# The first solve's base products ahead of the SSD stage's last products, its first inverses before the key weights

## The reference, cut to what matters

```python
xn = _rms_norm(h, pre_mix_norm[l])
proj = (xn @ w_in[l]).astype(jnp.float32)
y_ssd = _ssd_mixer(p_ssd, ...)       # chunks of 128; y * silu(z), then a norm by groups
y_rwkv = _rwkv7_mixer(p_rwkv, ...)   # the recurrence below
mix = jnp.concatenate([y_ssd, y_rwkv], axis=-1) @ w_out[l]
...
def step(S, inp):                    # _rwkv7_scan, 256 steps, 8 heads of 64
    sa = jnp.einsum("bhij,bhj->bhi", S, a_t)
    S = S * w_t[:, :, None, :] + sa[..., None] * b_t[:, :, None, :] + v_t[..., None] * k_t[:, :, None, :]
    return S, jnp.einsum("bhij,bhj->bhi", S, r_t)
```

## Time and profile before

| what | before |
|---|---|
| median of 3 runs | 737.87 us (737.47 to 738.0) |
| the profiled execution | 737.89 us |
| its span, first to last instruction | 736.1 us |
| TensorE busy | 725.6 us, 99% |
| VectorE busy | 563.6 us, 77% |
| ScalarE busy | 435.3 us, 59% |
| GpSimd busy | 49.4 us, 7% |
| granted TensorE clock, mean | 0.998 |

### The profile page before, as it was taken

The page is one execution under the profiler, slowest core; times in us unless marked ns, Lnnn a source line. Parts: engine busy times, 40 slices in busy tenths (PEclk is TensorE's granted clock), DMA queues, the critical chain, the costliest instruction groups (busy, mean ns, idle before and its releaser), DMA issues.

```text
span 736.1 us, 16703 instructions
## 1 busy us (share of the span) xinstructions
PE 725.6 (99%) x7176; PEld 592.3 (80%) x7176; DVE 563.6 (77%) x895; ACT 435.3 (59%) x689; POOL 49.4 (7%) x83
## 2 busy tenths in 40 slices
PE   9999999999999999999999999999999999999997
PEld 7888877888788888888878695898888888865553
DVE  5789978777789999997568787889685676762453
ACT  5699863425748666766557572487473755653342
POOL 0000133040020000000002000003003000000000
PEclk9999999999999999999999999999999999999999
DMA  9990205320666655565771732338335354566001
GB/s 316 394 410 10 113 19 219 129 88 31 231 232 224 218 181 180 225 225 177 280 292 36 288 138 112 116 126 333 116 124 219 106 211 170 203 229 234 24 1 58
DMA packets 67146, 129.51 MB, mean 176 GB/s; under 512 B 3968, under 2 KB 28032, under 8 KB 66816
## 3 DMA queue, kind: packets, MB, share of 16 engines
q1 hardware_dynamic: 66032, 126.07, 46.9%
q0 software_dynamic: 320, 1.67, 0.6%
q10 hardware_dynamic: 720, 0.70, 0.3%
HBM read 127.39 MB, written 1.05 MB: 174 GB/s over the span
## 4 chain that ended last, share of the span: by engine, by line
PE 91%; DVE 6%; issue 1%; ACT 1%; ACTq 0%; DVEq 0%
PE bank L626 44%; PE bank L748 14%; PE bank L3205 11%; PE bank L2531 3%; PE bank L1570 3%; PE bank L1551 2%; PE bank L883 1%; DVE arena L572 1%; PE bank L1829 1%; PE bank L902 1%; PE bank L2008 1%; DVE arena L614 1%; PE bank L828 1%; PE bank L2745 1%; PE bank L3028 1%
## 5 line engine op out<-in xcount | busy, mean ns | idle before, releaser
L626 PE MATMUL bank<-hg,arena 128*128 128x256 f16 x2496 | 275.0, 273 | 0.2 <-DVE hg L651 0.2
L626 PEld LDWEIGHTS bank<-hg,arena 128*128 128x128 f16 x2496 | 243.9, 98 | 30.5 <-issue 1.1
L572 DVE SCALAR_TENSOR_TENSOR arena<-ring,arena 128x1024 f16<-128x1024 f32 x150 | 175.6, 1226 | 59.1 <-ACT arena L540 59.1
L540 ACT ACTIVATE arena<-ring 128x1024 f16<-128x1024 f32 x150 | 146.7, 1044 | 86.8 <-PE bank L3205 37.6
L3205 PE MATMUL bank<-arena 128*128 128x512 f16 (+1 forms) x480 | 83.6, 336 | 0.0
L3205 PEld LDWEIGHTS bank<-arena 128*128 128x128 f16 x480 | 47.0, 98 | 36.1
L748 PE MATMUL bank<-arena 128*128 128x256 f16 x528 | 57.8, 273 | 0.0
L748 PEld LDWEIGHTS bank<-arena 128*128 128x128 f16 x528 | 51.7, 98 | 6.0
L559 DVE SCALAR_TENSOR_TENSOR arena<-ring,arena 128x2048 f16<-128x2048 f32 x22 | 50.4, 2292 | 0.7
L748 PE MATMUL bank<-mix,arena 128*128 128x256 f16 x384 | 42.2, 273 | 0.0
L552 ACT ACTIVATE arena<-ring 128x2048 f16<-128x2048 f32 x22 | 41.7, 1894 | 0.0
(11 more groups left out here) (420 smaller groups left out, 971.1 us busy)
## 6 DMA issues: line engine op xcount, KB each, us to landing
ring<-in_w_in_dram SPq DMA_DIRECT2D x12, 2048.0 KB, 8.9
ring<-in_ffn_w_up_dram SPq DMA_DIRECT2D x22, 1024.0 KB, 7.2
ring<-in_w_ff_dram SPq DMA_DIRECT2D x8, 2048.0 KB, 9.2
ring<-in_w_ff_dram SPq DMA_DIRECT2D x16, 1024.0 KB, 6.4
ring<-in_ffn_w_down_dram SPq DMA_DIRECT2D x11, 1024.0 KB, 5.2
ring<-in_w_out_dram SPq DMA_DIRECT2D x8, 1024.0 KB, 7.9
ring<-in_w_xk_dram SPq DMA_DIRECT2D x2, 2048.0 KB, 11.6
ring<-in_w_xv_dram SPq DMA_DIRECT2D x2, 2048.0 KB, 10.1
```

The lines of the kernel that those rows point to most:

```text
L540: nc.scalar.activation(quarter(halves_of(chunk)[0], chunk, q), quarter(slot(*chunk), chunk, q), ACT.Copy, scale=W_SCALE).then_inc(*mark("w ...
L572: nc.vector.scalar_tensor_tensor(quarter(halves_of(chunk)[1], chunk, q), quarter(slot(*chunk), chunk, q), W_SCALE, quarter(halves_of(chunk ...
L626: mm = nc.tensor.matmul(out_, weight[a][:, k, cols], src[:, k, b, :], start=(first and i == 0), stop=(last and i == 2), skip_group_check=True)
```

## The change

On TensorE, the base products of chunk 0 move from behind `products` to a place between z tile 3 and the SSD products of chunk 1, with three waits before them. On VectorE, all four memory tiles 4 to 7 come before z's eviction, the first inverses of both groups come before the low half of key quarter 0, and the negated blocks become a step of their own, "lower blocks", behind that low half. Level 0's product waits for that step too. In chunk 1 the order of VectorE's work stays as it was.

```diff
             for c in range(NC_):
                 if c:
                     pe_z_tile(pe, 3)
+                    pe.wait_ge(*at("k token-major"))
+                    pe.wait_ge(*at("ssd state out"))
+                    pe.wait_ge(*at("AT"))
+                    base_products(0)
                 for g in range(2):
                     pe.wait_ge(*at("ssd mt", c, g))
...
-            dve_mem_low16(dve, (4,))
+            dve_mem_low16(dve, (4, 5, 6, 7))
             dve_z(dve, 1)
-            dve_mem_low16(dve, (5, 6, 7))
+            for g in range(2):
+                dve_first_inverse(dve, 0, g)
             mem_low(dve, 0)
+            for g in range(2):
+                dve_lower_blocks(dve, 0, g)
...
             products(c, 0, BT, AT_, "LT bank")
-            if c == 0:
-                base_products(c)
             fill(0)
...
                     if n == 0:
                         pe.wait_ge(*at("LT", c, g))
+                        pe.wait_ge(*at("lower blocks", c, g))
...
+        def base_blocks(g):
+            return banks[3 * g + 1][:, 0:4 * BASE].rearrange("p (j n) -> p j n", j=4)
+
+        def dve_lower_blocks(dve, c, g):
+            if c:
...
+                return
+            dve.wait_ge(*at("ssd y", 1, 1))
+            nc.vector.tensor_scalar(LT32[g], base_blocks(g), -1.0, None, ALU.mult).then_inc(
+                *mark("solve_vector", "lower blocks", c, g))
+
+        def dve_first_inverse(dve, c, g, between=lambda: None):
+            st = sets[g]
+            dve.wait_ge(*at("blocks bank", c, g))
+            if c:
+                dve.wait_ge(*at("XT diagonal", 0, g))
+            nc.vector.tensor_tensor(st["XT"], base_blocks(g), over(const("pair32"), 4), ALU.mult).then_inc(
+                *mark("solve_vector", "XT pairs", c, g))
+            between()
+            dve.wait_ge(*at("XT pairs", c, g))
+            nc.vector.tensor_tensor(st["XT"], st["XT"], over(const("ident32"), 4), ALU.add).then_inc(
+                *mark("solve_vector"))
+            dve.wait_ge(*so_far("solve_vector"))
+            nc.vector.transpose(flat(st["X"]), flat(st["XT"])).then_inc(*mark("solve_vector", "X", c, g, 0))
+
         def dve_rwkv_chunk(dve, c):
-            for g in range(2):
...
+            if c:
+                for g in range(2):
+                    dve_first_inverse(dve, c, g, lambda: dve_lower_blocks(dve, c, g))
             for n, m in enumerate(LEVELS):
```

More of the change, by code:

```diff
@@ L2018, in even @@
             return v.rearrange("p (b two m) -> p b two m", two=2, m=m)[:, :, 0, :]
-        def dve_rwkv_chunk(dve, c):
-            for g in range(2):
[L2022 to L2042, removed]
@@ new lines, in base_blocks @@
+        def base_blocks(g):
+            return banks[3 * g + 1][:, 0:4 * BASE].rearrange("p (j n) -> p j n", j=4)
+        def dve_lower_blocks(dve, c, g):
+            if c:
+                nc.vector.tensor_tensor(
+                    LT64[g].rearrange("p j (two n) -> p j two n", two=2),
+                    base_blocks(g).unsqueeze(2).broadcast_to([P, 4, 2, BASE]),
+                    const("blocks64").rearrange("p (two n) -> p two n", two=2).unsqueeze(1).broadcast_to(
+                        [P, 4, 2, BASE]), ALU.mult).then_inc(*mark("solve_vector", "lower blocks", c, g))
+                return
+            dve.wait_ge(*at("ssd y", 1, 1))
+            nc.vector.tensor_scalar(LT32[g], base_blocks(g), -1.0, None, ALU.mult).then_inc(
+                *mark("solve_vector", "lower blocks", c, g))
```

## The result

The changed kernel takes 739.49 us (median of 13 runs, 739.03 to 741.27), the kernel before 737.87 (13 runs, 737.35 to 738.44): a ratio of 1.0026, 95% interval 1.0018 to 1.0033. By the medians it is slower by 1.62 us, and 739.6 was forecast. (The medians' quotient is 1.0022.

What follows compares the result with a forecast made beforehand. TensorE, busy 99% of the span, was taken as the bound, with VectorE on the chain from 101.15 to 107.25 us. Terms +0.61, +1.72, -0.18 and -0.39 gave +1.76 on 737.89: 739.65, about 739.6 as median; range 738.4 to 740.3.

Steps and rivals of the forecast that it cites:

- The step on which all hangs: VectorE's tile 5, issued behind GpSimd's r by k product, stands until 96.08 and takes about 2.5 us instead of 0.48.
- Rival A: VectorE's memory tiles do not stand behind GpSimd, so the kernel is not slower: -0.27 us, 737.6; chance 0.08.
- Rival B: VectorE keeps the port, GpSimd waits, and the first "plus identity" stands until 97.24: +0.88 us, 738.8; chance 0.12.
- Rival C: A later wait swallows part of the loss, or a term is too large: +0.5 to +1.4 us, 738.4 to 739.3; chance 0.12.
- Rival D: The 1.75 us wait costs TensorE its clock, half quarter 2.84 instead of 1.42: +1.4 us more, 741; chance 0.04.
- z +0.61: On VectorE, z's eviction comes behind the memory tiles instead of hidden under GpSimd's product: +0.61 us.
- inverses +1.72: On VectorE, both first inverses run ahead of the low half that TensorE's next product waits for: +1.72 us.
- the nearer hand-over -0.18: From the low half's end to TensorE's use of it takes 0.06 us instead of 0.24: -0.18 us.
- level 0 -0.39: TensorE's level 0 of both groups runs back to back, 0.73 us instead of 1.12: -0.39 us.
- packed: From 101.15 us on VectorE is busy for 5.91 of 6.05 us, so everything behind moves together by the shift.

Runs made afterwards that it cites:

- the tiles only: The kernel before, with only the three memory tiles 5 to 7 moved ahead of z's eviction: 739.10 us against 737.64, ratio 1.0026.
- the inverses only: The changed kernel with memory tiles 5 to 7 back behind z, so only base products and first inverses are early: 738.88 us against 737.64 for the kernel before.
- the low half first: The changed kernel with key quarter 0's low half put ahead of the first inverses on VectorE: 739.07 us against 737.75 for the kernel before, ratio 1.0017.
- the product twice: The changed kernel with GpSimd's product r*k' issued twice in a row: 743.55 us against 737.75 for the kernel before, ratio 1.0087.

## Why the prediction was right

All steps are counted from tile 4's start (0.48 later in the profile after). z's eviction was forecast 3.70 us behind it and came 3.69 behind. The two inverses were put at 1.72 and took 1.72. The low half was to end at 7.24 and ended at 7.19. TensorE's wait for z was put at 0.35 and was 0.40; that for the low half at 1.75 and was 1.58. The level-0 run of 64 began at 8.67, where 8.72 was forecast. The shift of the second key quarter was put at 1.76 and was 1.70, and 1.62 of it showed in the median.

The step on which all hangs, that tile 5 stands until GpSimd's product is through, held as written, with 2.58 us for a tile against the 2.5 named. That the product is the cause was shown from both sides: held back, the four tiles take 1.67; issued twice, a second tile is held for 2.57.

Rival A (the tiles are not held) fell at the 2.58 us. What it described came true when the product was moved, -0.38 us on the interval where it had -0.27. Rival B (VectorE keeps the port) fell at the same tile, and the "plus identity", where it put the wait, took its plain 0.29. Rival C (swallowed later) did not take place in the stretch; 0.08 us between profile and medians is within the scatter of the runs. Rival D (the clock) did not come in the median, nor in the profiled execution (granted clock 1.00 in the whole stretch). But 3 of the 13 executions took 740.18 to 741.27 us at a mean clock of 0.996, so 0.04 was too little for what single executions do.

Two things the prediction had less well. It named the sum's terms as z +0.61, inverses +1.72, the nearer hand-over -0.18 and level 0 -0.39. The runs group them as +0.59, +1.51 and -0.40, the second being 1.72 less 0.18, so they agree to 0.03. And it called everything from 101.15 us on packed, which holds for VectorE and hid that TensorE has stalls there, two in the kernel before (0.54 at 103.39 and 0.44 at 106.95), that lie under its waits for VectorE: for the forecast they did not count, for the attempts to gain more they were the new bound.

## What to carry to other kernels

Before work is moved into an engine's idle time, look at what the other engines do in it. VectorE's 1.05 us were idle only for instructions that GpSimd's product does not hold: while the product ran, z's eviction from PSUM took its plain 0.69, and a memory tile of 0.48 with two inputs in SBUF took 2.58. And when something is made early, ask what is now late behind it in the same queue: the inverses were ready 1 us sooner, but the instruction that they were put ahead of was the one TensorE wanted first.

## What the runs showed of the hardware that was not expected

**The clock fell in some executions of the kernels in which TensorE waits one to two and a half microseconds.** Mean granted clocks of 0.996 or less came in 3 of 13 executions of the changed kernel (waits of 0.40 and 1.58 us), 1 of 11 with the tiles only (1.09), 1 of 11 with the inverses only (1.44), 4 of 10 with the low half first (0.39, and a stall of 1.11) and 4 of 5 with the product twice (2.49 and 1.57). In the six versions without such a wait there was none in 66, and in the kernel before 1 in 79. One in 11 can't be told from 1 in 79; the 13 in 50 of the five kernels together can. The length of the wait does not order them: 1.09 and 1.44 us gave 1 of 11 each, and the low half first had 4 of 10 with no wait for another engine over 0.39 ahead of the fall in its profile. The three of the changed kernel took 740.18, 740.27 and 741.27 us, the ten others have a median of 739.43 (one of them, 740.48, is long at a mean clock of 1.0). The mean misses short falls: the one execution of the product twice that is not counted has 0.998, as many undisturbed ones, and is the one profiled here. Its windows show what TensorE did before:

```profile
98.00:100.00 2.00, 0.00 (x0) 0.00 (x0) 2.00 (x3) 0.00 (x0) 0.88 (x1) 1.00 0.00 0
100.00:102.00 2.00, 1.16 (x16) 1.00 (x16) 1.86 (x8) 1.78 (x2) 0.00 (x0) 1.00 0.00 0
102.00:104.00 2.00, 0.95 (x5) 0.70 (x6) 1.39 (x3) 1.99 (x6) 0.00 (x0) 0.74 0.01 4
104.00:106.00 2.00, 2.00 (x29) 1.19 (x31) 0.00 (x0) 1.75 (x4) 0.00 (x0) 0.50 0.04 8
```

and its price on one group of 12 products, 2.74 us instead of 1.48:

```profile
103.05 2.74 PE L1558 MATMUL bank<-xk,sqs 128*128 128x256 f16 x12 [1.57 <-DVE sqs L1536]
```

From 1.26 us here and 0.22 in the level behind it comes the part of this run that the held tiles don't explain: to level 1 it was 19.00 against 15.44 with the change, 3.56, of which 2.10 are tiles. The fall came at about 103 us, at the end of the second of two waits close together (2.49 and 1.57): TensorE was busy for 0 and 1.16 of 2 us in the two windows before and for 0.95 in the one with the fall, and the clock was back at about 106.4. That the waits cause the fall is argued from these counts and two profiles; no run varied the waits alone.
